# Hybrid decoder step on one core: the last down-projection block with stationary activations and a norm per token tile

## What is computed

```python
x = x + (silu(gate) * value) @ w_down        # w_down: 5632 x 2048
y = x * rsqrt(mean(x * x, axis=-1) + EPS) * final_norm_w
```

## Time and profile before

| | us |
|---|---|
| median of 3 runs | 1651.55 (1651.45 to 1652.08) |
| the profiled execution | 1651.99 |
| its span in the trace | 1650.3 |
| PE busy | 1628.6 |
| DVE busy | 1041.2 |
| ACT busy | 629.0 |

### The profile page before, as it was taken

How to read it: one execution, slowest core, us unless ns; L and a number is a source line. 1 busy time by engine, 2 the same in 40 slices (tenths; PEclk the granted TensorE clock), 3 DMA queues, 4 the chain that set the end, 5 groups by cost and what they waited for, 6 DMA issues and landing times.

```text
span 1650.3 us, 30926 instructions
## 1 busy us (share of the span) xinstructions
PE 1628.6 (99%) x12899; PEld 1580.3 (96%) x12899; DVE 1041.2 (63%) x1691; ACT 629.0 (38%) x810; POOL 237.7 (14%) x370
## 2 busy tenths in 40 slices
PE   8999999999999999999999999999999999999998
PEld 7999989988998998999999999999999999999997
DVE  5676678656544455776666666666666666666665
ACT  6554334432343343643333333333333333333334
POOL 1122342122212022310000000101010101010004
PEclk9999999999999999999999999999999999999998
DMA  8454355435857467454445444444544444445442
GB/s 241 139 154 120 105 154 155 115 103 159 260 173 248 129 211 227 134 160 146 150 145 160 142 154 153 150 145 153 153 147 148 154 151 145 152 142 158 148 154 84
DMA packets 231243, 256.64 MB, mean 156 GB/s; under 512 B 9444, under 2 KB 220966, under 8 KB 231104
## 3 DMA queue, kind: packets, MB, share of 16 engines
q1 hardware_dynamic: 217856, 220.10, 43.4%
q0 software_dynamic: 10560, 33.29, 6.5%
q10 hardware_dynamic: 2688, 1.27, 0.3%
HBM read 243.50 MB, written 12.69 MB: 155 GB/s over the span
## 4 chain that ended last, share of the span: by engine, by line
PE 95%; DMA 2%; DVE 1%; issue 1%; SPq 0%; ACT 0%; POOL 0%; DVEq 0%; POOLq 0%; ACTq 0%
PE ps_proj L1781 23%; PE ps_proj L1783 22%; PE ps_proj L1782 22%; PE ps_small L1781 6%; PE ps_small L1783 6%; PE ps_small L1782 6%; PE ps_small L1823 2%; DMA w_raw<-in_w_in_dram 1%; DMA k_pages<-in_cache_k_dram 1%; PE ps_small L1965 0%; PE ps_small L2055 0%; DMA state_s<-in_state_gdn_dram 0%; PE ps_small L1955 0%; PE ps_small L2161 0%; PE ps_small L2143 0%
## 5 line engine op out<-in xcount | busy, mean ns | idle before, releaser
L1781 PE MATMUL ps_proj<-x_hi,w_hi 128*128 128x320 f32 x2432 | 765.6, 315 | 1.0 <-DVE x_lo L1299 0.5
L1783 PE MATMUL ps_proj<-x_hi,w_lo 128*128 128x320 f32 x2432 | 751.8, 309 | 0.0
L1782 PE MATMUL ps_proj<-x_lo,w_hi 128*128 128x320 f32 x2432 | 751.8, 309 | 0.0
L821 ACT ACTIVATE w_hi<-w_raw 128x1024 fp32r<-128x1024 f32 x408 | 431.8, 1058 | 723.4 <-PE ps_proj L1783 528.9
L1191 DVE TENSOR_TENSOR w_lo<-w_raw,w_hi 128x1024 fp32r<-128x1024 f32 x408 | 498.1, 1223 | 300.2 <-ACT w_hi L821 299.8
L1781 PEld LDWEIGHTS ps_proj<-x_hi,w_hi 128*128 128x128 f32 x2432 | 457.1, 188 | 15.0 <-issue 10.5
L1782 PEld LDWEIGHTS ps_proj<-x_lo,w_hi 128*128 128x128 f32 x2432 | 457.3, 188 | 0.3
L1783 PEld LDWEIGHTS ps_proj<-x_hi,w_lo 128*128 128x128 f32 x2432 | 456.9, 188 | 0.0
L1781 PE MATMUL ps_small<-hid_hi,w_hi 128*128 128x320 f32 x704 | 218.0, 310 | 0.0
L1783 PE MATMUL ps_small<-hid_hi,w_lo 128*128 128x320 f32 x704 | 217.6, 309 | 0.0
L1782 PE MATMUL ps_small<-hid_lo,w_hi 128*128 128x320 f32 x704 | 217.5, 309 | 0.0
(11 more groups left out here) (348 smaller groups left out, 1207.4 us busy)
## 6 DMA issues: line engine op xcount, KB each, us to landing
w_raw<-in_w_up_dram SPq DMA_DIRECT2D x176, 512.0 KB, 3.5
w_raw<-in_w_in_dram SPq DMA_DIRECT2D x112, 512.0 KB, 4.1
w_raw<-in_w_down_dram SPq DMA_DIRECT2D x88, 512.0 KB, 3.5
w_raw<-in_w_out_dram SPq DMA_DIRECT2D x32, 512.0 KB, 3.9
k_pages<-in_cache_k_dram POOLq DMA_DIRECT2D x32, 256.0 KB, 3.6
v_pages<-in_cache_v_dram POOLq DMA_DIRECT2D x32, 256.0 KB, 4.3
state_s<-in_state_gdn_dram POOLq DMA_DIRECT2D x10, 512.0 KB, 5.6
out_ss_dram<-state_s POOLq DMA_DIRECT2D x8, 512.0 KB, 4.5
```

What stands on the lines that cost most here:

```text
L821: act.activation(whi[:, slot], raw[:, slot], ACT.Copy).then_inc(hi_done, 1)
L1781: pe.matmul(o, hi, rhs_hi[:, k0 + kk_, :], start=first and kk_ == 0, stop=False)
L1782: pe.matmul(o, hi, rhs_lo[:, k0 + kk_, :], start=False, stop=False)
L1783: ins = pe.matmul(o, lo, rhs_hi[:, k0 + kk_, :], start=False, stop=last and kk_ == CQ - 1)
```

## The change

In the last block the hidden activations are stationary (128 tokens of one 128-feature tile), and 512 columns of weights move. A chunk is now 128 rows x 1024 columns, four for the columns 0 to 1023 (`d` = 0 to 3), then four for 1024 to 2047. The result comes out in token rows. The 64 sample tokens are stationary as 128 columns, hi beside lo (`hs`, copied by ACT and DVE), so two products give all four combinations, and the lower half of the result is moved by ACT (`low_moved`) and added by a second sum. The residual `xres` of the block before is turned to token rows (`xtok`) during the block, in bursts between the products (`turned_rows`, 17 of them with the new rows; two banks in turn, evicted by `turned_out`). DVE adds PSUM to `xtok` (`added`), ACT squares with a running sum (`square_of`), and each of the three token tiles gets its own root, scale and two transfers, tile 0 first, then the samples, then tile 1. The final weight comes as a row, broadcast to all partitions by a transfer of POOL, which multiplies the first 1024 columns by it; DVE does so for the rest in its scale. The buffers `facc` and `hf` have moved; the sums of squares on PE are gone.

```diff
+TURNS = ([("x", t, q) for q in range(2) for t in range(3)] + [("new", 0, r) for r in range(5)]
+         + [("x", t, q) for q in range(2, 4) for t in (0, 2, 1)])
...
SP
-                load(d % RING, down_source(NB - 1, d), None)
+                k0 = (NB - 1) * 512 + d % 4 * P
+                load(d % RING, w_down[k0:k0 + P, d // 4 * 1024:d // 4 * 1024 + 1024], None, wide(raw, d % RING))
...
ACT
+            def scaled(t, count):
+                rows = rows_of(t)
+                out = yo[rows, t, 0:1024]
+                act.wait_ge(fin["r"], count)
+                act.wait_ge(fin["w"], count)
+                act.activation(out, out, ACT.Copy, scale=sm("rsx", rows.stop, t, t + 1)).then_inc(fin["ya"], 1)
 
             for d in range(3, 8):
                 hi_part(c + d, d % RING, (c + d) // RING)
...
+                if d < 7:
+                    for i in range(3 * (d - 3), 3 * (d - 3) + 3):
+                        turned_out(i)
...
+            act.wait_ge(mm_done, down_start(NB - 1) + 4)
+            low_moved()
+            for t, turns in ((0, (12, 13)), (1, (14,)), (2, (15, 16))):
+                act.wait_ge(fin["x"], t + 1)
+                square_of(t, 0, 1024, t)
+                for i in turns:
+                    turned_out(i)
             for j in range(2):
...
+                act.wait_ge(fin["x"], 4 + j)
+                square_of(0, 1024 + 512 * j, 512, 3 + j)
+            root_of(0, 4, 5, 1)
+            act.wait_ge(fin["acc"], 5)
+            low_moved()
+            scaled(0, 1)
+            act.wait_ge(fin["x"], 6)
+            square_of(2, 1024, 1024, 5)
+            root_of(2, 5, 6, 2)
+            act.wait_ge(fin["x"], 7)
+            square_of(1, 1024, 512, 6)
+            scaled(2, 2)
+            act.wait_ge(fin["x"], 8)
+            square_of(1, 1536, 512, 7)
+            root_of(1, 7, 8, 3)
+            scaled(1, 3)
...
DVE
+            def added(t, c0, bank, moved=None):
+                rows = rows_of(t)
+                x = xtok[rows, t, c0:c0 + bank.shape[1]]
+                if moved is None:
+                    tt(x, bank[rows], x, ALU.add).then_inc(fin["x"], 1)
...
+            for d in range(5):
+                lo_part(c + d + 3, (d + 3) % RING)
+            dve.wait_ge(fin["tok"], 6)
+            for t in range(2):
+                dve.wait_ge(fin["acc"], t + 1)
+                added(t, 0, two_banks(psB, 2 * t))
+            dve.wait_ge(mm_done, down_start(NB - 1) + 4)
+            added(2, 0, two_banks(psA, 2), 1)
+            dve.wait_ge(fin["wn"], 16)
+            dve.wait_ge(fin["sq"], 1)
+            chain(mean_before(0, 0, sm("so", P, 0, 1)))
+            dve.wait_ge(fin["tok"], len(TURNS))
             for j in range(2):
...
+                dve.wait_ge(fin["acc"], 3 + j)
+                added(0, 1024 + 512 * j, psB[:, j, :])
...
+            scaled(0, 1)
+            dve.wait_ge(fin["acc"], 5)
+            added(2, 1024, two_banks(psA, 2), 2)
+            dve.wait_ge(fin["acc"], 6)
+            added(1, 1024, psB[:, 2, :])
+            scaled(2, 2)
+            dve.wait_ge(fin["sq"], 7)
+            mean_on(1, 6, sm("so", P, 1, 2), sm("ro", P, 2, 3)).then_inc(fin["pre"], 1)
+            dve.wait_ge(fin["acc"], 7)
+            added(1, 1536, psB[:, 3, :])
+            dve.wait_ge(fin["x"], 8)
+            scaled(1, 3)
...
PE
+            def token_products(out, k, t, w_h, w_l):
+
+                h_, l_ = (x[:, (NB - 1) % 2, k, P * t:P * t + P] for x in (hhi, hlo))
+                pe.matmul(out, h_, w_h, start=k == 0, stop=False)
+                pe.matmul(out, h_, w_l, start=False, stop=False)
+                return pe.matmul(out, l_, w_h, start=False, stop=k == 3)
...
+            for d in range(4):
+                pe.wait_ge(lo_done, c + d + 1)
+                for t in range(2):
+                    if d == 0:
+                        pe.wait_ge(f["add"], 8 * (NB - 1) + t + 1)
+                    for x, w_ in enumerate(halves(d)):
+                        ins = token_products(psB[:, 2 * t + x, :], d, t, *w_)
+                    if d == 3:
+                        ins.then_inc(fin["acc"], 1)
+                    turned_rows(3 * d + t)
                 if d == 0:
...
+                    pe.wait_ge(fin["hs"], 2)
+                for x, w_ in enumerate(halves(d)):
+                    ins = sample_products(psA[:, 2 + x, :], d, *w_)
+                ins.then_inc(mm_done, 1)
+                turned_rows(3 * d + 2)
+
+            for k in range(4):
+                pe.wait_ge(lo_done, c + k + 5)
+                if k == 0:
+                    pe.wait_ge(fin["x"], 1)
+                for x, w_ in enumerate(halves(4 + k)):
+                    ins = token_products(psB[:, x, :], k, 0, *w_)
+                    if k == 3:
+                        ins.then_inc(fin["acc"], 1)
+                turned_rows(12 + k)
+            pe.wait_ge(fin["x"], 3)
+            pe.wait_ge(fin["low"], 1)
+            for k in range(4):
+                for x, w_ in enumerate(halves(4 + k)):
+                    ins = sample_products(psA[:, 2 + x, :], k, *w_)
+                if k < len(TURNS) - 16:
+                    turned_rows(16 + k)
+            ins.then_inc(fin["acc"], 1)
+            for x in range(2):
+                for k in range(4):
+                    ins = token_products(psB[:, 2 + x, :], k, 1, *halves(4 + k)[x])
+                ins.then_inc(fin["acc"], 1)
...
POOL
+            pool.wait_ge(mm_done, down_start(NB - 1))
+            pool.dma_start(wfin[:, :], I["final_norm_w"].rearrange("(a n) -> a n", a=1).broadcast_to([P, DM])).then_inc(fin["wn"], 16)
+            pool.wait_ge(fin["tok"], 11)
             pool.dma_start(O["fcp"][0, 0].rearrange("r (f c) -> f r c", c=P), frow[0:88, 0:2, :]).then_inc(fin["no"], 16)
...
+            for count, t in ((1, 0), (2, 2), (3, 1)):
+                rows = rows_of(t)
+                pool.wait_ge(fin["x"], 3 if t == 2 else t + 1)
+                pool.tensor_tensor(yo[rows, t, 0:1024], xtok[rows, t, 0:1024], wfin[rows, 0:1024], ALU.mult).then_inc(fin["w"], 1)
```

More of the change, by code:

```diff
@@ L654, in build @@
     f = {k: sem("ffn_" + k) for k in ("evac", "pad", "conv", "silu", "h", "hhi", "hlo", "add", "tap")}
-    fin = {k: sem("fin_" + k) for k in ("sq", "sqs", "ss", "ms", "mt", "mr", "r", "w", "t", "ev", "half", "x7", "y0", "y1", "out", "nt", "ne", "no")}
+    fin = {k: sem("fin_" + k) for k in ("hs", "turn", "tok", "acc", "low", "x", "sq", "pre", "mr", "r", "wn", "w", "ya", "yv", "out", "no")}
     links = {"V": 0, "A": 0, "G": 0}
@@ L1135, in last_tile_square @@
[L1135 to L1145, removed]
+            last = (NB - 1) % 2
@@ new lines, in _, with turned_out @@
+            act.wait_ge(f["hhi"], 2 * NB)
+            act.activation(hs[:, :, 0:NS], hhi[:, last, :, SEQ:TOK].bitcast(F32), ACT.Copy).then_inc(fin["hs"], 1)
+            def turned_out(i):
+                act.wait_ge(fin["turn"], i + 1)
+                kind, t, q = TURNS[i]
+                bank = psA[:, i % 2, :]
+                if kind == "x":
+                    rows = rows_of(t)
+                    act.activation(xtok[rows, t, 512 * q:512 * q + 512], bank[rows], ACT.Copy).then_inc(fin["tok"], 1)
+                else:
+                    m_ = min(4, 18 - 4 * q)
+                    act.activation(frow[0:88, 4 * q:4 * q + m_, :],
+                                   bank[0:88, 0:m_ * P].rearrange("p (j c) -> p j c", j=m_), ACT.Copy).then_inc(fin["tok"], 1)
@@ new lines, in square_of, with low_moved, root_of @@
+            def square_of(t, c0, width, j):
+                rows = rows_of(t)
+                if j:
+                    act.wait_ge(fin["sq"], j)
+                return act.activation(squared[rows, 0:width], xtok[rows, t, c0:c0 + width], ACT.Square,
+                                      accum_out=sm("tmp", rows.stop, j, j + 1)).then_inc(fin["sq"], 1)
+            def low_moved():
+                act.activation(lower[0:NS, :], two_banks(psA, 2)[NS:P], ACT.Copy).then_inc(fin["low"], 1)
+            def root_of(t, j, squares, count):
+                n = unit(t)[0]
+                act.wait_ge(fin["sq"], squares)
+                act.wait_ge(fin["pre"], count)
+                act.activation(sm("ssx", n, t, t + 1), sm("tmp", n, j, j + 1), ACT.Sqrt, scale=1.0 / DM,
+                               bias=sm("ro", n, count - 1, count)).then_inc(fin["mr"], 1)
@@ L1742, in _ @@
[L1742 to L1765, removed]
+            def added(t, c0, bank, moved=None):
+                rows = rows_of(t)
+                x = xtok[rows, t, c0:c0 + bank.shape[1]]
+                if moved is None:
+                    tt(x, bank[rows], x, ALU.add).then_inc(fin["x"], 1)
+                else:
+                    chain(tt(x, bank[rows], x, ALU.add))
+                    dve.wait_ge(fin["low"], moved)
+                    tt(x, lower[0:NS, :], x, ALU.add).then_inc(fin["x"], 1)
@@ L2251, in turn_y, with turned_rows @@
-            def turn_y(q):
```

(10 more changed lines are left out.)

194 lines of the change are left out of this document (66 added, 128 removed).

## The result

The changed kernel takes 1657.52 us (median of 8 runs, 1656.66 to 1659.65) against 1651.84 (8 runs) for the kernel before in the same session: ratio 1.0032, 95% interval 1.0024 to 1.0041. It is slower by 0.32%. The profiled execution took 1657.88 with a span of 1656.2.

A forecast was written before the change was run, and what follows sets the result against it. TensorE was taken to fill the span, busy 1628.6 of 1650.3 us. Plus 4.3 us, or 6.3 with the clock's fall, against the median 1651.55 gave 1655.9 or 1657.9; forecast 1657.5, range 1654.0 to 1661.0.

The forecast's parts named there:

- Products: Last block on PE: 128 products of 512 columns at 0.227 us each, 29.0 us, 0.9 more than now.
- First half: PE's first 1024 columns: 64 products 14.5 us, eleven bursts 5.4, end 1622.6; twelfth burst to 1623.1.
- Stall: Between the halves PE waits 4.4 us for DVE's sum of tile 0, behind eviction, w_hi and w_lo.
- Clock: PE's clock falls in the gap; about 5 us of work at the lower level, 2.0 us lost.
- Second half: PE's columns 1024 to 2047: tile 0 7.5 us, samples 4.1, tile 1 two groups at 2.72 each.
- Tail: From PE's last product to the last scaled row: 4.9 us against 6.6 now, decided by DVE's order.
- Outputs: From the last scaled row to the end: only the last two transfers, 1.05 MB, 5.06 us.
- GpSimd's three products cost nothing: Final-weight products on GpSimd, 2.8 us each, done at 1637.6, before ACT wants the last at 1648.3.
- B: Last block: the stall occurs but the clock holds; 1655.9 us (1654.7 to 1657.3), chance 0.28.
- C: Last block: PE's wait between the halves is hidden, not slower; 1652.5 us, chance 0.13.
- D: Tail at its upper bound, or lower clock for much of the second half; above 1660.5 us, chance 0.07.
- E: Last block faster: products much closer, from 0.13 us each on, span ending at 1648.2; chance 0.02.

The follow-up runs named there:

- e1: Changed kernel with DVE summing the first halves of tiles 0 and 1 before the last w_lo; 1653.86 us, ratio to before 1.0011.
- e2: Changed kernel with PE filling the stall with 18 idle products of 512 columns; 1655.45 us.
- e3: Changed kernel with DVE waiting for the 15th eviction instead of the 17th before the second half of tile 0; 1656.38 us.
- e6: e1 with GpSimd's first product held back until all three first-half sums are done; 1652.27 us, ratio to before 0.9997.
- e9: e7 with the three final-weight products on DVE and none on GpSimd; 1649.82 us, ratio to before 0.9981.
- e8: e7 with DVE and ACT taking the last part of tile 1 before scaling the samples; 1655.15 us.
- e7: e6 with DVE's wait for the 15th eviction from e3; 1652.47 us.
- e4: Changed kernel with GpSimd's first product waiting until all three first-half sums are done; 1659.48 us in one run.

## Why the prediction was right

The forecast was 1657.5, the median is 1657.52. So close a hit is partly luck. The working came to 1657.9 and was rounded down, and the terms were off in opposite ways: 0.6 us too much for the first half, 0.2 too little for the second, 0.6 too little for the tail, 0.9 too much for the outputs. That makes 0.7 too much in all: 6.3 us were forecast between the two spans, 5.6 were measured. The mechanism, a stall of 4.4 us and a fall of the clock, is the one that the runs show. By its steps:

- **Products.** 0.227 each was assumed. They stand 0.232 apart in the first half of the block, 0.227 near its end (1645.99 to 1646.22). The rule of the Trainium skill (TensorE: Matmul & The Clock Gate, "Wait — 56ns, not 53.3ns?"), 215.7 ns, is too low here, as it was at 320 columns.
- **First half.** 20.4 us forecast with the twelfth burst, 19.8 measured (1602.96 to 1622.75; a burst of four takes 0.35, not 0.42). The bursts were priced a little high. The number of transposes before was miscounted too: by the kernel's loops 54 stand ahead of the last product and 12 behind it, not 50 and 16. No term of the sum hangs on that.
- **Stall.** 4.4 us forecast; 1622.75 to 1627.11 is 4.4, of which the profile counts 4.12 as idle. The four steps stand in the rows as named. e1 shows it is DVE's order that makes it: one call moved, and the stall is gone.
- **Clock.** It fell 2.8 us after PE's last work, 1.6 before PE restarted, and PE then worked at the lower level for 5.2 us, until 1632.3 ("about 5" was forecast). The price assumed was 2.0; e2 gives 2.1 to 2.4. The Trainium skill's warning about idle gaps between bursts of matmuls (TensorE: Matmul & The Clock Gate, "Why this matters for your kernels") agrees with this profile.
- **Second half.** 17.1 + 2.0 forecast, 19.3 measured (1627.11 to 1646.45, the last start plus 0.227).
- **Tail.** 4.9 us from the last product to the last scaled row forecast, 5.5 measured. Every square with a running sum is followed by a read of 0.19, and the root takes 0.29 instead of 0.21. DVE takes the last part up 2.2 us after 1646.45; the prediction says 1.7, though its own times (1644.6 and 1646.46) give 1.9. e3 shows that its queue matters.
- **Outputs.** 5.1 forecast, 4.2 measured. Scaling the bytes down from the earlier trace rows kept too much: the start and landing of six transfers aren't those of two.
- **GpSimd's three products cost nothing.** True for the changed kernel, by luck of place. The prediction named only their duration (2.8 each, 2.38 measured) and missed that they hold DVE up. They kept a sum back by 2.0 us in DVE's idle time, and they cost 1.6 us in e1 (against e6; 2.1 by the distance from the kernel before), where PE waited for that sum. The trace of before already showed such a hold; its rows stand in the last section.
- **Rivals.** B (stall, clock holds) has 4.3 us over the kernel before; e2, which makes that case, is 3.3 over. C (no stall) has 0.9 over; e6, once the second wait was gone as well, is 0.4 under, 0.4 over by the profiled blocks. Their absolute times, 1655.9 and 1652.5, look closer to 1655.45 and 1652.27 than that, because the kernel before was 0.6 to 1.1 us slower in those sessions than in the prediction's. D and E are excluded by the rows: at the upper level the products stand 0.227 to 0.232 apart, the scale takes 1.28 and not 1.73, and the lower level holds for 5.2 of the 19.3 us of the second half.

What isn't parted: how much of the remaining cost is columns and how much bursts. From PE's first to its last product the block takes 36.8 us in e9 (1600.80 to 1637.54) against 34.85 before, though nothing waits there any more. What makes e9 the faster one is that the norm per tile shortens what follows, 9.1 us against 12.7.

## What to carry to other kernels

When work is put between the halves of a block, walk the queue of each engine from the instruction that frees the buffer: here a sum of 1.2 us waited behind a conversion for a chunk that nobody needed yet, and the 4 us of PE's idleness took another 2 in clock. An engine's idle time that seems free may be what hides a hold-up between two others; after closing one gap, read again what took its place. And the order and spacing in which tiles finish are also those of the transfers: the last pair of e8, 1.2 us behind the pair before it, took 6.2 us to the end, that of e7, 3.05 us behind, took 4.4.

## What the runs showed of the hardware

**DVE and GpSimd.** While GpSimd ran 1024-column products, DVE instructions with two inputs in SBUF stood until it was through: a sum of 1.22 us took 3.20 or 5.47, and a one-column mean of 0.16 took 2.24 or 3.09, while sums with one input in PSUM kept their 1.2. The Trainium skill (GPSIMD Engine Reference, "1. Specifications") says that GpSimd shares its SBUF interfaces with DVE and names contention with instructions of two SBUF inputs; the rows agree, and show its size here: even one column waited for the whole product.

The trace of before, read again, shows two more things. DVE, then GpSimd:

```profile
1615.93 0.68 DVE L1719 TENSOR_SCALAR x_normed<-x_res,params_t 128x320 f32<-128x320 f32 x2
1618.39 2.53 DVE L1719 TENSOR_SCALAR x_normed<-x_res,params_t 128x320 f32<-128x320 f32 x2
1621.57 1.21 DVE L1191 TENSOR_TENSOR w_lo<-w_raw,w_hi 128x1024 fp32r<-128x1024 f32 x1
...
1621.73 1.79 POOL L2479 TENSOR_TENSOR root<-root,squares 128x320 f32<-128x320 f32 x1
1624.53 0.88 POOL L2479 TENSOR_TENSOR root<-root,squares 128x320 f32<-128x320 f32 x1
```

A pair of instructions with one tensor and one column as inputs took 2.53 us instead of 0.68, and ended 0.2 us behind GpSimd's sum of 1619.84. So a second whole tensor isn't needed for the hold. And it goes both ways: a sum of GpSimd that began beside DVE's w_lo took 1.79 instead of 0.88.

Issuing transfers doesn't hold DVE by itself: in e6 the sum ran beside GpSimd's issues in 1.22. In e1 it was held from 1628.07 on, while GpSimd's product shows only from 1630.08 on, behind the issues. e1 and e6 differ in one wait alone, the one that releases that product, so the early release brings the hold. But w_lo, also with two inputs in SBUF, took its usual 1.23 at 1625.68 of e1, when the product had been released already. At which point behind the release the hold begins is open.

**The clock.** The same stall of 4.12 us doesn't cost the same each time. Windows of e3, where PE restarts at 1627.38, and then of e4, where it restarts at 1629.54:

```profile
1627.00:1627.40 0.40, 0.02 (x1) 0.05 (x1) 0.40 (x2) 0.13 (x1) 0.40 (x2) 1.00 0.72 175
1627.50:1627.90 0.40, 0.40 (x2) 0.31 (x3) 0.40 (x1) 0.40 (x1) 0.40 (x2) 0.50 0.54 113
...
1629.50:1629.90 0.40, 0.36 (x2) 0.35 (x3) 0.40 (x1) 0.40 (x1) 0.40 (x1) 1.00 0.42 113
1630.10:1630.50 0.40, 0.40 (x2) 0.33 (x1) 0.40 (x2) 0.40 (x2) 0.40 (x1) 0.50 0.24 92
```

There the clock fell only when PE was at work again, 4.4 and 4.9 us after its last work, and not 2.8 as in the changed kernel. It came back at 1630.8 and 1633.4, so that PE worked at the lower level for 3.4 us in both, against 5.2. In e1, whose gap was 2.2 us, it read 1.00 from 1631.00 to 1633.50 and behind the gap. The three profiles are of one stall, and why the fall comes at different times isn't shown.
